# A feed-forward input product by seven half-size block products, and an output product in a stage of its own

## The reference, cut to what matters

```python
x = x + ga1 * ((g_a * y_a + g_b * y_b) @ w['w_out'])
h2 = _rms(x, w['norm2_g']) * (1.0 + sc2) + sh2
u_gate, u_val = jnp.split(h2 @ w['w_ffn_in'], 2, axis=-1)
x = x + ga2 * ((jax.nn.silu(u_gate) * u_val) @ w['w_ffn_out'])
```

## Time and profile before

| | before |
|---|---|
| median of 3 runs | 2063.2 us (2061.85 to 2069.53) |
| profiled execution, its own time | 2080.14 us |
| its span, first to last instruction | 2078.2 us |
| PE busy | 1962.9 us, 94% of the span |
| DVE / ACT / POOL busy | 1164.2 / 678.7 / 152.4 us |
| mean granted TensorE clock | 0.961 of full |

### The profile page before, as it was taken

The page is one execution under the profiler, slowest core; times in us unless marked ns, Lnnn a source line. Parts: engine busy times, 40 slices in busy tenths (PEclk is TensorE's granted clock), DMA queues, the critical chain, the costliest instruction groups (busy, mean ns, idle before and its releaser), DMA issues. The chain is left out here.

```text
span 2078.2 us, 35223 instructions
## 1 busy us (share of the span) xinstructions
PE 1962.9 (94%) x13248; PEld 1871.6 (90%) x13248; DVE 1164.2 (56%) x2531; ACT 678.7 (33%) x1273; POOL 152.4 (7%) x190
## 2 busy tenths in 40 slices
PE   5889999999996899998999999999999999999997
PEld 4658999999995888888898999999999999999997
DVE  4944333333245677777765546655656555555555
ACT  5623334322223566666562133311111010101011
POOL 1442100001300000001100000000000000000000
PEclk8898998999997899999899999999999999999999
DMA  9876554421101000000003531121202121211102
GB/s 311 269 214 195 173 161 126 148 88 52 52 1 67 1 1 1 1 1 1 1 1 127 178 122 59 34 61 30 61 30 61 30 61 30 61 36 55 40 0 82
DMA packets 151760, 157.13 MB, mean 76 GB/s; under 512 B 15859, under 2 KB 132483, under 8 KB 151604
## 3 DMA queue, kind: packets, MB, share of 16 engines
q1 hardware_dynamic: 140076, 130.73, 20.6%
q0 software_dynamic: 4656, 16.40, 2.4%
q10 hardware_dynamic: 6912, 8.46, 1.1%
HBM read 139.33 MB, written 18.32 MB: 76 GB/s over the span
## 5 line engine op out<-in xcount | busy, mean ns | idle before, releaser
L1877 DVE SCALAR_TENSOR_TENSOR l_x2T<-tail_bank,g_modT,l_x2T 128x344 f32<-128x344 f32 (+1 forms) x528 | 265.3, 566 | 101.5 <-PE tail_bank L1614 101.3
L1614 PE MATMUL tail_bank<-l_wo 128*128 128x344 f32 x1584 | 270.2, 319 | 1.8 <-DVE late_total_s L1883 1.8
L1614 PEld LDWEIGHTS tail_bank<-l_wo 128*128 128x128 f32 x1584 | 252.7, 188 | 2.0 <-issue 2.0
L1448 ACT ACTIVATE l_act<-tail_bank 128x344 f32<-128x344 f32 x66 | 30.2, 457 | 524.7 <-PE tail_bank L1596 524.7
L884 PE MATMUL nsa_out<-zs_z,nsa_probT 128*128 128x64 f32 (+1 forms) x1344 | 178.6, 279 | 5.8 <-DVE zs_z L1040 5.6
L884 PEld LDWEIGHTS nsa_out<-zs_z,nsa_probT 128*128 128x128 f32 x1344 | 171.5, 201 | 7.6 <-DVE zs_z L1040 7.5
L1596 PE MATMUL tail_bank<-late_words_hi,l_uhi 128*128 128x344 f32 x528 | 170.2, 322 | 3.3 <-DVE late_words_lo L1780 3.3
L1596 PE MATMUL tail_bank<-late_words_hi,l_ulo 128*128 128x344 f32 x528 | 169.7, 321 | 0.0
L1596 PE MATMUL tail_bank<-late_words_lo,l_uhi 128*128 128x344 f32 x528 | 169.6, 321 | 0.0
L1596 PE MATMUL tail_bank<-late_words_hi,l_wo 128*128 128x344 f32 x528 | 169.1, 320 | 0.0
L1596 PE MATMUL tail_bank<-late_words_lo,late_wo 128*128 128x344 f32 x528 | 169.1, 320 | 0.0
(11 more groups left out here) (504 smaller groups left out, 4325.8 us busy)
## 6 DMA issues: line engine op xcount, KB each, us to landing
mod_wr<-in_w_ada SPq DMA_DIRECT2D x24, 1024.0 KB, 5.4
kin_kin<-in_cache_kv SPq DMA_DIRECT2D x64, 256.0 KB, 3.5
late_gate<-in_w_ffn_in SPq DMA_DIRECT2D x22, 512.0 KB, 5.8
l_raw_o<-in_w_ffn_out SPq DMA_DIRECT2D x22, 512.0 KB, 3.6
late_raw<-in_w_ffn_in SPq DMA_DIRECT2D x22, 512.0 KB, 5.5
gate_d<-dec_gate ACTq DMA_DIRECT2D x48, 172.0 KB, 3.3
late_gate<-gate_d SPq DMA_DIRECT2D x8, 1032.0 KB, 5.3
dec_vin<-in_cache_kv SPq DMA_DIRECT2D x64, 128.0 KB, 2.2
```

The lines of the kernel that those rows point to most:

```text
L1448: act.activation(sg[(j + c) % 2], pg[(j + c) % 2][:, 0:TCH], ACT.Silu).then_inc(silu_done, 1)
L1614: mm = pe.matmul(po[u % 4][:, 0:TCH], w[j][:, k * P:(k + 1) * P], a[j][:, tok(c)], start=(q == 0), stop=(q == 2))
L1877: mm = dve.scalar_tensor_tensor(out=here, in0=po[u % 4][:, 0:part_w(c)], scalar=g.modT[:, 5 * KD + k, NDEC:NC9], in1=here, op0=ALU.mult, o ...
```

## The change: what it does

The input product is written as a 2 x 2 block product: the weights of two blocks of hidden channels (`v` and `v + 11`) by the lower and upper 4 blocks of input channels, and the activations by the lower and upper 4 blocks of channels and the first and second 516 tokens (`TH`). Eight block products would make it; the changed kernel makes it by seven, from sums and differences of blocks, and adds the seven results up to the four output blocks. A unit `u` is one such product (gate for even `u`, value for odd), 22 units in all. A block product is a set: 4 blocks of channels deep, 2 x 258 tokens (`SUB`), 3 matmuls each for hi and lo, so 24 matmuls of 258 columns in two PSUM banks; 154 sets, 3,696 matmuls.

- **Weight sums.** POOL makes four sums `S` for each unit (`weight_sums`, 4 instructions of 128 x 512). ACT and DVE split the seven weight sets of a unit (`hi_set`, `lo_set`), one set for each product that PE works on, for the next unit, in 8 slots.
- **Token sums.** Once, behind the second norm, POOL makes four sums `T1` to `T4` for each of 4 pairs of blocks (`token_sums`, 16 instructions of 128 x 516), ACT their hi (`hi_t`) and DVE their lo parts (`lo_t`). PE's third product (`n == 2`) waits for all 16. The scaled activations now overwrite `x2T`, which is stored to the device memory first (`x2_stored`), and DVE waits for that store ahead of `scaled`.
- **Result sums.** For each unit ACT copies two products out of PSUM, DVE adds five, and POOL adds two more (`product_sums`); silu and the product with the value follow on ACT and POOL (`gated_values`), now on 516 columns from on-chip memory. The activations go to the device memory (`acts_stored`).
- **Output product.** It is a separate last stage of six groups `G` (a chunk of 344 tokens and 4 of the 8 output blocks). In a group PE adds over all 22 hidden blocks in PSUM, 12 matmuls of 344 columns for each piece of `w_ffn_out` (128 x 512): 132 pieces, again 1,584 matmuls. Each piece is loaded and split anew, so `w_ffn_out` is read three times; the activations are read back, split once for each chunk, and `x2T` is read back from the device memory by 8 transfers behind piece 10. DVE adds a group's result into `x2T` once (`accumulated`), 24 times in all in place of 528.

```diff
+                def unit_weights(u):
+                    if u < 1:
+                        sp.wait_ge(wo_split, KD)
+                    elif u < 2:
+                        sp.wait_ge(h_ready, len(h_jobs))
+                        sp.wait_ge(t_sum, 16)
+                    else:
+                        sp.wait_ge(set_ready, set_of(u - 2, 6) + 1)
+                        sp.wait_ge(s_ready, u - 1)
+                    for b in range(2):
+                        f = (u // 2 + b * NFH) * P + u % 2 * D_FF
+                        sp.dma_start(raw_u[u % 2][b], w_u[:, :, f:f + P]).then_inc(u_in[u % 2], 16)
...
+                    sp.wait_ge(comb, comb_at(c * KD + n1 - 1))
+                    sp.dma_start(x2_d[:, n0:n1, tok(c)], x2T[:, n0:n1, tok(c)]).then_inc(x2_out[c], 16)
...
+                for n in range(7, NPIECE):
+                    output_weights(n)
+                    if m < NF or (m < 3 * NF and n >= (2 * (m // NF) - 1) * NF + m % NF + (1 if m % NF < 6 else 7)):
+                        activations(m)
+                        m += 1
+                    if n == 10:
+                        sp.wait_ge(a_out, 32 * NFH)
+                        for k in range(KD):
+                            sp.dma_start(x2T[:, k, :], x2_d[:, k, :]).then_inc(x2_in, 16)
...
+                def weight_sums(u):
+                    one, two = raw_u[u % 2]
+                    pool.wait_ge(u_in[u % 2], 32 * (u // 2) + 32)
+                    if u == 0:
+                        pool.wait_ge(xT_sb, 2 * TT + 1)
+                    else:
+                        pool.wait_ge(set_ready, set_of(u - 1, 6))
+                    S = [sums_u[:, i] for i in range(4)]
+                    pool.tensor_tensor(S[0], two[:, 0:4], two[:, 4:8], ALU.add).then_inc(s_step, 1)
+                    pool.tensor_tensor(S[2], one[:, 0:4], two[:, 0:4], ALU.subtract)
+                    pool.wait_ge(s_step, 2 * u + 1)
+                    pool.tensor_tensor(S[1], S[0], one[:, 0:4], ALU.subtract).then_inc(s_step, 1)
+                    pool.wait_ge(s_step, 2 * u + 2)
+                    pool.tensor_tensor(S[3], one[:, 4:8], S[1], ALU.subtract).then_inc(s_ready, 1)
...
+                def token_sums(k):
+
+                    first, second = slice(0, TH), slice(TH, NTOK)
+                    t11, t12, t21, t22 = (x2T[:, r, half] for r in (k, k + 4) for half in (first, second))
+                    done = lambda n: 4 * k + T_ORDER.index(n) + 1
+                    reuse = lambda n: pool.wait_ge(t_ready, 4 * (k - 1) + T_ORDER.index(n) + 1) if k else None
+                    pool.wait_ge(hs_st, 3)
+                    pool.wait_ge(t_done, 2 * KD + 2 * k + 2)
+                    reuse("T3")
+                    pool.tensor_tensor(tf["T3"], t22, t12, ALU.subtract).then_inc(t_sum, 1)
+                    pool.wait_ge(t_sum, done("T3"))
+                    reuse("T2")
+                    pool.tensor_tensor(tf["T2"], tf["T3"], t11, ALU.add).then_inc(t_sum, 1)
+                    reuse("T1")
+                    pool.tensor_tensor(tf["T1"], t12, t11, ALU.subtract).then_inc(t_sum, 1)
+                    pool.wait_ge(t_sum, done("T2"))
+                    reuse("T4")
+                    pool.tensor_tensor(tf["T4"], t21, tf["T2"], ALU.subtract).then_inc(t_sum, 1)
+
...
+                def product_sums(u):
+                    dest = (sg, av)[u % 2]
+                    pool.wait_ge(u2, u + 1)
+                    pool.wait_ge(p5_copied, u + 1)
+                    dest_free(u, a12)
+                    pool.tensor_tensor(dest[0][:, halves[1]], u2_sb, p5_sb, ALU.add).then_inc(u2p5, 1)
+                    pool.wait_ge(u3, u + 1)
+                    dest_free(u, a22)
+                    pool.tensor_tensor(dest[1][:, halves[1]], u3_sb, p5_sb, ALU.add).then_inc(c22, 1)
...
+                weight_sums(0)
+                for k in range(4):
+                    token_sums(k)
+                for u in range(NUNIT):
+                    if u + 1 < NUNIT:
+                        weight_sums(u + 1)
+                    product_sums(u)
+                    if u % 2 == 1:
...
+            def hi_set(act, u, i):
+
+                n = set_of(u, i)
+                act.wait_ge(u_in[u % 2], 32 * (u // 2) + 32)
+                if i in (2, 3, 4, 5):
+                    act.wait_ge(s_ready, u + 1)
+                set_free(act, n)
+                act.activation(set_slot(n)[0], set_source(u, i), ACT.Copy).then_inc(set_hi, 1)
...
-            def hidden(pe, f, j, before=None):
-
-                pe.wait_ge(u_ready, f + 1)
-                for c in range(3):
-                    n = f * 3 + c
-                    b = (j + c) % 2
-                    if before is None:
-                        pe.wait_ge(h_ready, (c + 1) * KD)
-                    pe.wait_ge(a_done, n + 1)
-                    for v, (banks, full) in enumerate(((pg, gate_full), (pv, val_full))):
-                        for k in range(KD):
-                            for q, (w, h) in enumerate(((uhi, h_hi), (ulo, h_hi), (uhi, h_lo))):
-                                mm = pe.matmul(banks[b][:, 0:TCH], w[j][:, v * KD + k, :], h[:, k, tok(c)],
-                                               start=(k == 0 and q == 0), stop=(k == KD - 1 and q == 2))
-                            if before is None and (c, v, k) == (0, 0, 6):
-                                squares_summed(pe, 2)
-                        mm.then_inc(full, 1)
-                        if before is not None:
-                            output(pe, before, 1 - j, 2 * c + v)
...
+                for u in range(NUNIT):
+                    for i in range(7):
+                        n = set_of(u, i)
+                        pe.wait_ge(set_ready, n + 1)
+                        if n >= 4:
+                            pe.wait_ge(evicted[(n - 4) % 7], (n - 4) // 7 + 1)
+                        elif n == 0:
+                            pe.wait_ge(xT_sb, 2 * TT + 1)
+                            pe.wait_ge(h_ready, 2 * KD)
+                        elif n == 1:
+                            pe.wait_ge(comb, comb_at(21))
+                        elif n == 2:
+                            pe.wait_ge(comb, comb_at(23))
+                            pe.wait_ge(t_ready, 16)
+                        else:
+                            pe.wait_ge(mean, 3)
+                            pe.wait_ge(prod, 6 + BR_ALL)
+                        if n == 5:
+                            pe.wait_ge(h_ready, len(h_jobs))
+                        w_hi, w_lo = set_slot(n)
+                        for sub in range(2):
+                            out = bank[:, PAIRS[n % 4] + sub, 0:SUB]
+                            for k in range(4):
+                                hi, lo = right[i](k, slice(sub * SUB, (sub + 1) * SUB))
+                                for q, (w, h) in enumerate(((w_hi, hi), (w_lo, hi), (w_hi, lo))):
+                                    mm = pe.matmul(out, w[:, k, :], h, start=(k == 0 and q == 0), stop=(k == 3 and q == 2))
...
+                        mm.then_inc(p_full, 1)
...
+                for G in range(6):
+                    banks_free(G)
+                    c = G // 2
+                    for i in range(NF):
+                        n = G * NF + i
+                        pe.wait_ge(set_ready, 7 * NUNIT + n + 1)
+                        if G % 2 == 0:
+                            pe.wait_ge(a_ready, c * NF + i + 1)
...
+                        w_hi, w_lo = piece_slot(n)
+                        for j in range(4):
+                            for q, (w, a) in enumerate(((w_hi, a_hi), (w_lo, a_hi), (w_hi, a_lo))):
+                                mm = pe.matmul(bank[:, F_BANKS[G % 2][j], 0:TCH], w[:, j * P:(j + 1) * P], a[i], start=(i == 0 and q == 0),
+                                               stop=(i == NF - 1 and q == 2))
+                        mm.then_inc(f_full, 1)
...
+            def lo_set(dve, u, i):
+
+                n = set_of(u, i)
+                hi, lo = set_slot(n)
+                dve.wait_ge(set_hi, n + 1)
+                dve.tensor_tensor(lo, set_source(u, i), f32(hi), ALU.subtract).then_inc(set_ready, 1)
...
+                    dve.wait_ge(x2_out[c], (16, 16, 128)[c])
...
+                def lo_t(k):
+                    for i, n in enumerate(T_ORDER):
+                        dve.wait_ge(t_hi_done, 4 * k + i + 1)
+                        hi, lo = t_hi[n][:, k, :], t_lo[n][:, k, :]
+                        if n == "T3":
+                            dve.scalar_tensor_tensor(out=lo, in0=tf[n], scalar=ds_k[:, k:k + 1], in1=f32(hi), op0=ALU.add,
+                                                     op1=ALU.subtract).then_inc(t_ready, 1)
...
+                def u3_summed(u):
+                    dve.wait_ge(p_full, in_order(u, 4))
+                    dve.wait_ge(u2, u + 1)
+                    if u:
+                        dve.wait_ge(c22, u)
+                        dve.wait_ge(c21, u)
```

(8 more changed lines are left out.)

677 lines of the change are left out of this document (442 added, 235 removed).

## The result

| | before | after |
|---|---|---|
| median, 20 runs each | 2071.0 us (2061.85 to 2084.51) | 2058.68 us (2047.79 to 2065.98) |
| ratio, 95% interval | | 0.9941 (0.9925 to 0.9956) |
| profiled execution, its span | 2078.2 us | 2054.3 us |
| first feed-forward product | 1302.4 | 1290.9 |
| from there to the end | 775.8 | 763.4 |

The account below looks back on a forecast made before the run. PE's matmuls, number times distance, were taken to bound the feed-forward part. Terms -62.5 + 35.9 + 3 + 0.9 = -22.7 us gave span 2055.5 for 2078.2, and 2040.5 us against the median 2063.2; range 2019 to 2068.

Parts of the forecast that it names:

- input product: Feed-forward input stage: 3,696 matmuls of 258 columns at 118 ns replace 3,168 at 157.4 ns, 62.5 us less.
- start: PE's wait before the third set for split token sums, until 1347.8: 35.9 us more (22 to 41).
- output stage: Matmuls as now, 249.3 us; one uncovered wait, near piece 11: 3 us more (0 to 8).
- end: Behind the last product: four blocks to add, then 16 transposes, last store about 6.3 us behind: 0.9 us more.
- the read-back of `x2T`: Output stage: 4.2 MB issued 7.5 us in take 14 to 16 us and delay piece 11, 3 us more.
- The other end: Lower bound of the wait before the third set, with POOL's sums not stopped by DVE: third set at 1334.0.
- The price of a matmul: Input stage: 258 columns cost 118 ns a matmul, bounds 115.3 to 121.6 ns.
- Start short: Rival, third set: DVE's instructions slip in without stopping POOL, set starts at 1334, total 2027 us; chance 0.10.
- Hand-overs between sets: Rival, input stage: hand-overs between 154 sets cost 0.15 us each, 23 us, total 2063; chance 0.10.
- POOL the bound of the units: Rival, units: POOL's 16 instructions take over 41.7 us in two units; at 2.8 us each, 2097; chance 0.11.
- Transfers hold back groups 1 and 3: Rival, output stage: landings of 8 us, a piece every 2.35 us, 44 pieces cost 20 us: 2061; chance 0.12.
- Hidden and indeed hidden: Stores of `x2T` ahead of scaling, SP's unit loads, and ACT's and DVE's splits in units: covered, cost 0.

Follow-up runs that it names:

- after_again: The changed kernel run once more with no edit: median 2055.15 us, ratio 0.9935 to the kernel before.
- spread: Changed kernel with the 8 read-back transfers of `x2T` issued singly behind every third piece, 11 to 32: 2052.47 us, 0.9897 to the kernel before.
- noread: Changed kernel without the read-back of `x2T`, so the output lacks the residual: 2049.72 us, ratio 0.9887 to the kernel before.
- nolo: Changed kernel with DVE's lo parts of token sums over 8 of 516 columns, PE taking hi instead: 2050.75 us, 0.9896 to the kernel before.
- eighth: Changed kernel with PE making the seventh block product of each unit twice, 528 more matmuls: 2119.78 us, ratio 1.0232 to the kernel before.
- pool2: Changed kernel with POOL making one weight sum three more times in each unit, results unused: 2061.33 us, ratio 0.9957 to the kernel before.
- order: Changed kernel with output pieces 7, 8 and 9 issued between the activation loads: 2058.57 us, ratio 0.9943 to the kernel before.

## Why the prediction came out half right

The direction held, and so did the mechanism (PE's matmuls bound the stage, and the new sums cost one stop at the start); the range held the time. The size did not: 2040.5 predicted, 2058.7 measured. Of these 18.2 us, 7.8 come from the base. I was given three runs of before with a median of 2063.2; over 20 runs it is 2071.0. The other 10.4 are the change itself, -22.7 predicted and -12.3 measured. By the terms of the sum:

| term | predicted | measured | how |
|---|---|---|---|
| input product | -62.5 | -56.6 | 3,696 x 119.6 ns = 442.0, less 498.6 |
| start | +35.9 | +30.0 | third set 39.5 us behind the first product, predicted 45.4 |
| output stage | +3 | +11.8 | 268.7 us, where the sum left 753.1 - 478.2 - 15.0 = 259.9 |
| end | +0.9 | +2.3 | tail 16.4 us, 14.1 before |
| sum | -22.7 | -12.5 | |

**The step that failed is the read-back of `x2T`.** The prediction said "the 4.2 MB of `x2T` issued behind piece 10, some 7.5 us into the stage", landing 14 to 16 us later, with piece 11 split at 24.5 and 3 us of waiting. (24.5 less 20.8 is 3.7, not 3.) The time of the transfer came out, by luck: from the issue at 1782.48 to the landing of piece 11 at 1798.6 are 16.1 us, but they moved some 6.3 MB at 389 GB/s, where 4.2 MB at 269 to 311 were taken; pieces and activations shared them. The issue did not come out: it came 13.3 us into the stage. I had taken piece 10 by PE's pace and left out what stands on SP's queue ahead of piece 7: twelve activation loads, with waits among them (1763.2 to 1775.2), and two stores that wait for POOL's last products (1777.6). So piece 11 was ready 30.8 us into the stage, 6.3 later than predicted, and PE, itself late by the stop at piece 7, came to it at 24.9 and not at 20.8. Experiments: 9.2 to 10.2 us are gone when the same bytes are spread, 8.2 to 9.2 when they are left out, and 4.2 MB against 2.1 at the same place stop PE for 6.0 to 6.6 against 1.5 us. The stop takes the clock with it, which the term had at nothing: by the table under after_again, the 10.2 us between the first trace and spread are 6.2 of idle time and 4.0 of slower matmuls, the 9.2 between after_again and spread 7.6 and 1.7. The earlier stop, 2.0 us ahead of piece 7, wasn't in the sum at all; 1.6 us of it stay in noread and spread.

**The start, a mis-sized term.** The place, the releaser (`lo_t`) and the start of the sums (9.3 us behind the first product, 9.4 predicted) came out; the third product was 5.9 us early. The prediction let POOL stand still for every DVE instruction, by a row in which DVE's partner took 2.28 us. With partners of 0.7 us a sum and a lo part take 1.7 us together, where 1.27 + 0.74 = 2.01 was assumed: most sums are 0.45 us longer for it and a lo part up to 0.8, but they run side by side. From the first sum to the end of the last are 28.6 us (1300.2 to 1328.8), where the turns had 34.3; the 28.6 hold 1.7 us of waiting for a buffer that the prediction didn't have. The other end, POOL without DVE, was given as 31.6 us behind the first product (1334.0) and is 32.4 in nolo, where DVE does little beside it. The Trainium skill, "Advanced Engine Details and Errata", section "GPSIMD Details", has the two engines share a read and a write interface. The runs agree that they take time from each other (1.27 to 1.72 us for a sum, 0.69 to 1.22 for a lo part), and not with full turns. The clock behind the stop cost what was taken: 478.3 - 39.5 - 3,648 x 0.1196 = 2.5 us, predicted 2.3; in after_again it is 3.4.

**The price of a matmul, a mis-sized term.** 119.6 ns is within the bounds (115.3 to 121.6) and 1.6 over the value taken; times 3,696 it is 5.9 us. These two errors cancel, and the input stage came out at 478.3 us for 478.2. That is luck, and says nothing for either term. The formula of the Trainium skill, "TensorE: Matmul & The Clock Gate", section "Back-to-back issue gap", gives 110 ns for a matmul alone; both long windows, in which each matmul has its load (119.6 and 119.7), disagree with it, as the earlier trace rows did.

**The end.** 1.4 us more than predicted, but not where the prediction looked. Timeline of the changed kernel:

```profile
2040.40 3.08 PE L1958 MATMUL tail_bank<-g_ident,l_x2T 128*128 128x128 f32 x16 [2.52 <-DVE l_x2T L2271]
...
2044.22 0.35 SPq L1450 DMA_DIRECT2D out_y_s<-late_gate  x1
```

The last product ends at 2037.9, so the last store is issued 6.3 us behind it, as predicted. From there to the end of the span are 10.1 us, where before had 8.7 (from 2069.55 to 2078.2). The clock behind the wait isn't the cause: in after_again the transposes take 1.94 us at the full clock, the last store is issued after 5.5 us, and the tail is 16.4 us all the same. The cause stays open.

**The rivals.** *Start short* fell: it needed 31.6 us, which only nolo (32.4) comes near; but the measured 39.5 lies between it and the forecast's 45.4, so it was right in part. *Hand-overs between sets* fell: the window of 402 us holds 140 of them without idle time, and a distance across one is 0.4 ns longer than one inside a set, where the rival needed 150; eighth prices a set at 2.87 to 2.91 us, 24 matmuls of 119.6 ns. *POOL the bound of the units* fell, but pool2 shows that its chain had little to spare, by my estimate some 3.5 us (5.1 us of added sums, less the first stop of 1.6). *Transfers hold back groups 1 and 3*: there are no stops behind the first group in any trace. The loss was of this kind, but in group 0, and from a burst.

**Hidden and indeed hidden:** the store of `x2T` ahead of the scaling, SP's loads of the units, and ACT's and DVE's splits in the units. PE has no idle time there, and DVE's first scaled block (1299.0) follows its small instructions without a wait.

## What to carry to other kernels

A transfer that must be made but isn't urgent is priced by what stands behind it in its queue, not by its bytes: find how much time the buffered loads cover, and issue it in portions under that. To place it in time, walk the issuing queue with its own waits, not the pace of the engine that consumes. Before work is put on an idle POOL to run beside DVE, ask what DVE alone would take: here PE stood still for 26.5 us with the 16 sums and 16 lo parts on DVE alone, and for 31.9 with the two together.

## What was unexpected in the hardware

- Beside POOL even a DVE instruction of 8 columns took 545 ns on average (nolo), where two of them with POOL idle took 0.21 us each (nolo, 1313.0), and one of 336 columns 1066 where it takes 563 alone. Both engines lose: POOL goes from 1.27 to 1.72 us.
- Matmuls of 258 columns with a load each come to 119.6 and 119.7 ns in two kernels, 0.464 ns a column, where 324 and 344 columns gave 0.456 and 0.458: what lies between 258 and the 112 ns of 128 columns only the three distances of 256 show.
- Removing a stop of 2 us ahead of a longer one gave nothing (order). With the longer one gone it gave 0.5 to 1.1 us, which is within the scatter of a stage.
- Behind the same stop of 31.90 us the clock came back some 2 us later in one trace than in the other (16 and 11 matmuls in the same 2 us), at a price of 0.9 us; in the output stage that price differed by 2.4 us. A wait's cost is its length and a varying stretch at 1.2 GHz behind it.
